# Attention, end of a head: the k-steps of r laid one by one between the samples' short products and behind their state products

## The chip, the cores and the metric

One core of one Trainium2 chip runs the whole program. The metric is the device time of one execution in microseconds. TensorE multiplies matrices into PSUM, VectorE and ScalarE work on SBUF and PSUM, GpSimd on SBUF, and SyncE issues most of the transfers. Each engine has its own queue of instructions, worked off in order; engines wait for each other by semaphores.

## The reference

A decoder layer runs for 1024 prompt tokens and for 8 samples of 8 tokens each. Its mixer holds a gated linear attention with 4 heads (key width 128, value width 256); a feed-forward part with product keys (PEER) gathers experts from memory and takes most of the time. What the changed stretch computes, cut from the reference:

```python
def step(s, inp):                       # one chunk of a head
    qi, ki, vi, gi = inp
    cum = jnp.cumsum(gi, axis=2)
    o_inter = jnp.einsum('bhcd,bhde->bhce', qi * jnp.exp(cum), s)
    ...                                 # scores with decay, inside the chunk
    o = o_inter + jnp.einsum('bhij,bhje->bhie', scores, vi)
    s_new = exp(last) * s + jnp.einsum('bhjd,bhje->bhde', ki * jnp.exp(last - cum), vi)
    return s_new, o
o = rms_norm(o, gla_norm_w)             # per head
o = o.reshape(bsz, t, GLA_DV) * jax.nn.silu(r)     # r = h @ w_in[:, r columns]
```

## The kernel before

`heads_phase` is a loop over the 4 heads. The 1088 tokens lie in 9 tiles: 8 of 128 prompt tokens, and a ninth (t = 8) with the 64 tokens of the samples. All work of a head on TensorE stands in one written order: the projections of q, k and v, the tile loop, and the end of the head. One more projection, r (256 output rows in two halves e, over 1088 tokens), isn't needed until the end of the head. It is cut into 6 pieces (half e, 384, 384 or 320 tokens), each of 8 k-steps; a k-step is three products with one block of 128 channels (high with high, high with low, low with high; L546 to L548). The 48 k-steps are laid as fillers into gaps of the other work: the list FILL says how many go to each place, and `fill(j)` writes those of place j. Place 0 is ahead of the tile loop, places 1 to 8 are in `results` of tiles 0 to 7 (behind the products L572, ahead of the state product L579), place 9 is after the samples' output products, and place 10 is after that.

All pieces use one PSUM bank (bank 7). When a piece's eighth k-step is done, ScalarE copies the bank to SBUF (`emptied`, L674) and only then may the next piece begin (`r_out`). ScalarE's own order is written out too: for each tile the output copy (L686), then `emptied` of that place, then the copy of the transposed keys (L698) and the exponentials of a tile two further on (L681).

The end of a head runs as follows. TensorE computes the samples' output: for each half e a product with the scores (L611), then for each of the 8 samples a product of its own state, 128 by 128, with only 8 columns (L614). Then comes the last filler. Then 8 state products (L627), one per sample, into two banks in turn; VectorE updates the sample's state from each (L797). Then six products (L633) sum the squares of the output over the channels. ScalarE makes these squares (the two activations L704 and L705, 1088 columns each), after the last `emptied`. After the sums come a root and a sigmoid on ScalarE, and the normalised output on VectorE, while TensorE goes on to the next head's q. When a head's third piece of r is complete, GpSimd splits the next head's q weights into a high and a low part (L144, L146); the k weights wait for all six pieces.

At the end of the phase all engines meet in a barrier, and the next phase starts then.

Of the kernel before, what the change touches and what calls it, by code (L numbers as in the profile page):

```python
# [15 lines left out]
KD = D // P  # L16
SEQ = 1024
NSEQ, LSEQ = 8, 8
T = SEQ + NSEQ * LSEQ
NC = 1 + NSEQ  # L20
NT = -(-T // P)
# [42 lines left out]
def col(t):  # L64
    return t * P if t < 2 else EARLY if t == NT - 1 else LATE + (t - 2) * P
# [302 lines left out]
def heads_phase(nc, A, G):  # L368


    with Scope(nc, "gla") as sc:
# [41 lines left out]
        M = {n: sc.sem(n) for n in names}  # L413
# [3 lines left out]
        tiles = [(t, rows(t), 0 if t < NT - 1 else 1) for t in range(NT)]  # L417
        assert NT % 2
        PIECES = [(e, t0, n) for e in range(2) for t0, n in TB]
        FILL = [KD] + [KD // 2] * (NT - 1) + [0, KD]  # L420
        filled = [sum(FILL[:j]) for j in range(len(FILL) + 1)]
        assert filled[-1] == len(PIECES) * KD
        r_bank = lambda p: PS[:, 7, 0:PIECES[p][2]]
# [71 lines left out]
        def _(pe):  # L495
# [3 lines left out]
            for b, (t0, n) in enumerate(TB):  # L499
                for kk in range(KD):  # L500
# [3 lines left out]
                    last = nc.tensor.matmul(PS[0:RANK, b, 0:n], lw_lo[:, kk, :], hi, start=False, stop=(kk == KD - 1))  # L504
            last.then_inc(M["low_mm"], 1)
            pe.wait_ge(M["low_ready"], 1)
            with pe.Fori(0, H) as i:
# [8 lines left out]
                for t, n, _ in tiles:  # L516
                    last = nc.tensor.matmul(PS[:, t // 4, t % 4 * DK:(t % 4 + 1) * DK],
                                            low[:, col(t):col(t) + P], w_alpha[:, bass.ds(i * DK, DK)],
                                            start=True, stop=True)
# [3 lines left out]
                for t, n, _ in tiles:  # L523
# [3 lines left out]
                    for kk in range(KD):  # L527
# [3 lines left out]
                        last = nc.tensor.matmul(out, lo, w_hi[:, 2:4, kk, :], start=False, stop=(kk == KD - 1))  # L531
# [1 line left out]
                pe.wait_ge(M["z_abs"], 2 * i + 2)  # L533
                pe.wait_ge(M["g_ready"], 4 * i + 4)

                def fill(j):

                    for s in range(filled[j], filled[j + 1]):
                        p, kk = divmod(s, KD)
                        e, t0, size = PIECES[p]  # L540
                        if kk == 0:
                            if t0 == 0:
                                pe.wait_ge(M["low_part"], NW * i + 5 + e)
                            pe.wait_ge(M["r_out"], 6 * i + p + 1)
                        hi, lo = h_hi[:, kk, t0:t0 + size], h_lo[:, kk, t0:t0 + size]
                        nc.tensor.matmul(r_bank(p), w_hi[:, e, kk, :], hi, start=(kk == 0), stop=False)  # L546
                        nc.tensor.matmul(r_bank(p), w_hi[:, e, kk, :], lo, start=False, stop=False)
                        last = nc.tensor.matmul(r_bank(p), w_lo[:, e, kk, :], hi, start=False, stop=(kk == KD - 1))  # L548
                        if kk == KD - 1:
                            last.then_inc(M["r_mm"], 1)  # L550
# [35 lines left out]
                for t, n, kind in tiles:  # L586
# [7 lines left out]
                    for l in range(LV + 1):  # L594
                        lhs = K[:, l, 0:n] if l < LV else k[:, col(t):col(t) + n]
                        rhs = Q[:, l, 0:n] if l < LV else q[:, col(t):col(t) + n]
                        last = nc.tensor.matmul(PS[0:n, 3 + l // 4, l % 4 * P:l % 4 * P + n], lhs, rhs,
                                                start=True, stop=True)
# [11 lines left out]
                for e in range(2):  # L610
                    last = nc.tensor.matmul(PS[:, 6, e * P:e * P + n], v[0:n, t, e * P:(e + 1) * P],  # L611
                                            sT[0:n, 0:n], start=True, stop=False)
                    for s in range(NSEQ):
                        last = nc.tensor.matmul(PS[:, 6, e * P + s * LSEQ:e * P + (s + 1) * LSEQ],  # L614
                                                Ss[:, s, e * P:(e + 1) * P],
                                                Qc[:, t % 3, s * LSEQ:(s + 1) * LSEQ],
                                                start=False, stop=(s == NSEQ - 1))
                last.then_inc(M["o_mm"], 1)
                fill(NT + 1)
                pe.wait_ge(M["kts"], i + 1)  # L620
                pe.wait_ge(M["masked"], NT * i + NT)
                for s in range(NSEQ):

                    pe.wait_ge(M["st_out"], NST * i + NT - 1 + max(s - 1, 0))
                    if s == 1:
                        pe.wait_ge(M["o_out"], NT * i + NT)
                    nc.tensor.matmul(ST if s % 2 else PS[:, 4, 0:DV], kTs[:, s, :], v[0:n, t, :],  # L627
                                     start=True, stop=True).then_inc(M["st_mm"], 1)
                pe.wait_ge(M["sq_ready"], i + 1)
                pe.wait_ge(M["st_out"], NST * (i + 1))  # L630
                for b, (t0, n) in enumerate(TB):
                    for e, src in enumerate((q, k)):
                        last = nc.tensor.matmul(PS[:, 3 + b, 0:n], G["ones"][:, :], src[:, t0:t0 + n],  # L633
                                                start=(e == 0), stop=(e == 1))
# [3 lines left out]
        def _(act):  # L638
# [6 lines left out]
            with act.Fori(0, H) as i:  # L645
# [23 lines left out]
                def emptied(j):  # L669

                    for p in range(filled[j] // KD, filled[j + 1] // KD):
                        e, t0, size = PIECES[p]
                        act.wait_ge(M["r_mm"], 6 * i + p + 1 + 6)
                        nc.scalar.activation(r[:, e, t0:t0 + size], r_bank(p), ACT.Copy).then_inc(M["r_out"], 1)  # L674
                def exps(t, n, kind):
                    act.wait_ge(M["e_mm"], NT * i + t + 1)
                    if t >= 2:
                        act.wait_ge(M["qk"], 3 * (NT * i + t - 2) + 3)
                    src = PS[:, 0:3, 0:384].rearrange("p b (l i) -> p b l i", l=3)[:, :, :, 0:n]
                    dst = E[:, t % 2].rearrange("p (b l) i -> p b l i", l=3)[:, :, :, 0:n]  # L680
                    nc.scalar.activation(dst, src, ACT.Exp).then_inc(M["e_exp"], 1)  # L681
                def output(t, n, kind):
                    act.wait_ge(M["o_mm"], NT * i + t + 1)
                    if t == 0:
                        act.wait_ge(M["o_free"], i + 1)
                    nc.scalar.activation(o[:, :, col(t):col(t) + n],  # L686
                                         PS[:, 6, 0:2 * P].rearrange("p (e i) -> p e i", e=2)[:, :, 0:n],
                                         ACT.Copy).then_inc(M["o_out"], 1)
# [3 lines left out]
                for t, n, kind in tiles:  # L692
                    if t >= 1:
                        output(*tiles[t - 1])
                        emptied(t)
                        act.wait_ge(M["st_mm"], NST * i + t)
                    act.wait_ge(M["t_mm"], NT * i + t + 1)
                    nc.scalar.activation(kT[0:n, :], PS[0:n, 5, 0:DK], ACT.Copy).then_inc(M["t_out"], 1)  # L698
                    if t + 2 < NT:
                        exps(*tiles[t + 2])  # L700
                output(*tiles[NT - 1])
                emptied(NT + 1)
                act.wait_ge(M["o_out"], NT * i + NT)
# [9 lines left out]
        def _(dve):  # L713
# [8 lines left out]
            with dve.Fori(0, H) as i:  # L722
# [17 lines left out]
                for gg, _, hi, lo in parts:  # L740
                    nc.vector.tensor_tensor(lo, gg, hi.bitcast(F32), ALU.subtract).then_inc(M["g_ready"], 1)
# [1253 lines left out]
def hybrid_decoder(nc, A):  # L1995

    with Scope(nc, "all") as top:
# [5 lines left out]
        with Scope(nc, "stream") as route:  # L2003

            G["h_hi"], G["h_lo"] = route.sb("h_hi", [P, KD, T], F32R), route.sb("h_lo", [P, KD, T], F32R)
            condition_phase(nc, A, G)
            heads_phase(nc, A, G)
# [115 lines left out]
```

## Time and profile before

| what | value |
|---|---|
| median of 3 runs | 4596.62 us (4596.38 to 4607.99) |
| the profiled execution's own time | 4599.16 us |
| its span, first to last instruction | 4597.4 us |
| PE busy | 3297.1 us, 72% |
| DVE busy | 2489.0 us, 54% |
| POOL busy | 1649.2 us, 36% |
| ACT busy | 803.6 us, 17% |
| mean granted TensorE clock | 0.784 of full speed |

The span is the program on the core; 1.8 us of the execution's own time lie around it. PE is TensorE's products, PEld its weight loads, DVE VectorE, ACT ScalarE, POOL GpSimd. The attention phase lies between about 160 and 725 us of the span. The granted clock is 1.00 at 2.4 GHz and 0.50 at 1.2 GHz. A product in full fp32 stands in the trace as two records, one in the rounded format (the k-steps, for one) as one. Records of TensorE overlap, since the next begins before the one ahead has drained; so the cost of one is read from start to start, not from its length.

### The profile page before, as it was taken

To read this page: it belongs to the slowest core of one execution; us is meant where nothing else is said; L and a number is where in the kernel's file an instruction comes from. 1 tells how busy PE (TensorE), PEld (TensorE's weight loads), DVE (VectorE), ACT (ScalarE), POOL (GpSimd) and SP (SyncE) were. 2 spreads that over 40 slices of the span, in tenths; PEclk is the share of its full clock that TensorE was granted. 3 is DMA by queue.
4 is the path that set the end of the run, shared out by engine and by line. 5 is a ranking of instruction groups with operands and counts; after the bars stand their busy time and mean duration, and the time that the engine had idled before them with its cause. 6 is when DMAs were issued, how large, how long until landed. Compare 5 with 4: busy or idle time off the path is not lost. (4 is left out here: it accounts for less than half of the span.)

```text
span 4597.4 us, 46652 instructions
## 1 busy us (share of the span) xinstructions
PE 3297.1 (72%) x15679; PEld 1688.6 (37%) x15679; DVE 2489.0 (54%) x7735; ACT 803.6 (17%) x1284; POOL 1649.2 (36%) x1379
## 2 busy tenths in 40 slices
PE   8899997736388666686768676667766666666676
PEld 2798896736055342351145334124211111111110
DVE  2245553126764445587755454557686555555555
ACT  2232233332113112110013211211000100000000
POOL 1211103523255343453345444344333333333332
PEclk9999998968599777797889888679766666666666
DMA  7211103533789889899889898999899999999998
GB/s 277 72 58 48 38 29 124 178 116 110 284 341 384 315 319 394 336 386 353 344 353 399 340 369 357 386 357 381 345 393 378 402 407 403 408 411 408 416 411 352
DMA packets 243431, 1400.14 MB, mean 305 GB/s; under 512 B 30662, under 2 KB 47686, under 8 KB 100987
## 3 DMA queue, kind: packets, MB, share of 16 engines
q0 software_dynamic: 156672, 1140.92, 61.9%
q1 hardware_dynamic: 86522, 256.22, 15.4%
q8 instruction: 131, 2.15, 0.2%
q14 instruction: 106, 0.86, 0.1%
HBM read 1345.59 MB, written 51.43 MB: 304 GB/s over the span
## 5 line engine op out<-in xcount | busy, mean ns | idle before, releaser
L1057 DVE CUSTOM_DVE_ANT_0 peer_uv<-peer_uv,all_PS 128x512 f32<-128x512 f32 x2176 | 1436.4, 685 | 1163.3 <-DMA peer_uv<-in_uv,peer_idx 782.8
L996 PE MATMUL all_PS<-peer_hT,peer_sel 96*128 96x512 bf16 x2176 | 1005.8, 486 | 1032.5 <-DVE peer_halves L1057 850.2
L979 POOL DMA_INDIRECT peer_uv<-in_uv,peer_idx x1088 | 1045.9, 961 | 1738.5 <-PE all_PS L1015 1360.4
L996 PEld LDWEIGHTS all_PS<-peer_hT,peer_sel 96*128 96x128 bf16 x2176 | 203.3, 102 | 2004.6 <-DVE peer_halves L1057 1623.6
L1015 PE MATMUL all_PS<-peer_uv,peer_zw 128*32 128x512 f32 x4352 | 878.0, 857 | 2.7 <-DVE peer_zw L1077 2.7
L867 POOL TENSOR_TENSOR flow_w_lo<-flow_w,flow_w_hi 128x1024 fp32r<-128x1024 f32 (+1 forms) x204 | 459.2, 2256 | 489.4 <-ACT flow_w_hi L860 488.9
L1031 ACT ACTIVATE peer_ge<-peer_pre 128x4 f32<-128x4 f32 x272 | 55.7, 205 | 2057.6 <-DVE peer_pre L1063 2057.5
L887 PE MATMUL all_PS<-mix_h_hi,flow_w_hi 128*128 128x384 f32 (+1 forms) x672 | 279.1, 415 | 33.2 <-POOL flow_w_lo L867 31.6
L860 ACT ACTIVATE flow_w_hi<-flow_w 128x1024 fp32r<-128x1024 f32 (+1 forms) x204 | 203.7, 1004 | 435.3 <-DMA flow_w<-in_w_proj_a 113.3
L888 PE MATMUL all_PS<-mix_h_lo,flow_w_hi 128*128 128x384 f32 (+1 forms) x672 | 225.2, 335 | 0.0
L889 PE MATMUL all_PS<-mix_h_hi,flow_w_lo 128*128 128x384 f32 (+1 forms) x672 | 225.1, 335 | 0.0
L1015 PEld LDWEIGHTS all_PS<-peer_uv,peer_zw 128*32 128x32 f32 x4352 | 109.5, 128 | 282.1 <-issue 279.0
L887 PE MATMUL all_PS<-keys_h_hi,flow_w_hi 128*128 128x384 f32 (+1 forms) x384 | 173.7, 452 | 27.7 <-DVE keys_h_lo L1682 27.7
L1057 DVE DVE_READ_ACCUMULATOR2_ANT peer_halves<- 128x1 f32 x2176 | 179.6, 83 | 0.0
L887 PEld LDWEIGHTS all_PS<-mix_h_hi,flow_w_hi 128*128 128x128 f32 x672 | 133.0, 198 | 104.4 <-issue 71.3
L144 POOL CAST gla_w_hi<-gla_w 128x1024 fp32r<-128x1024 f32 x24 | 24.9, 1038 | 374.2 <-PE all_PS L548 288.8
L888 PEld LDWEIGHTS all_PS<-mix_h_lo,flow_w_hi 128*128 128x128 f32 x672 | 131.4, 195 | 6.4
L888 PE MATMUL all_PS<-keys_h_lo,flow_w_hi 128*128 128x384 f32 (+1 forms) x384 | 130.2, 339 | 0.0
L889 PE MATMUL all_PS<-keys_h_hi,flow_w_lo 128*128 128x384 f32 (+1 forms) x384 | 130.1, 339 | 0.0
L889 PEld LDWEIGHTS all_PS<-mix_h_hi,flow_w_lo 128*128 128x128 f32 x672 | 130.0, 193 | 0.0
L1405 PE MATMUL all_PS<-flow_w_hi,out_x_hi 128*128 128x256 f32 (+1 forms) x288 | 107.1, 372 | 21.3 <-DVE out_x_lo L924 18.4
L887 PEld LDWEIGHTS all_PS<-keys_h_hi,flow_w_hi 128*128 128x128 f32 x384 | 77.6, 202 | 83.8 <-issue 83.5
(290 smaller groups left out, 4699.8 us busy)
## 6 DMA issues: line engine op xcount, KB each, us to landing
cond_w<-in_w_ada SPq DMA_DIRECT2D x12, 2048.0 KB, 8.2
flow_w<-in_w_gate_ab SPq DMA_DIRECT2D x48, 512.0 KB
flow_w<-in_w_query SPq DMA_DIRECT2D x48, 512.0 KB
flow_w<-in_w_conv SPq DMA_DIRECT2D x36, 512.0 KB
peer_uv<-in_uv,peer_idx POOLq DMA_INDIRECT x1088, 10.1
gla_w<-in_w_heads SPq DMA_DIRECT2D x24, 512.0 KB, 4.2
flow_w<-in_w_proj_b SPq DMA_DIRECT2D x24, 512.0 KB
flow_w<-in_w_out SPq DMA_DIRECT2D x24, 512.0 KB
```

Source lines behind the costliest of these rows:

```text
L144: nc.gpsimd.tensor_copy(hi, raw).then_inc(high, 1)
L860: nc.scalar.activation(self.hi[:, i % self.pairs, 0:nk], self.raw[:, i % self.raws, 0:nk], ACT.Copy).then_inc(self.high, 1)
L867: nc.gpsimd.tensor_tensor(self.lo[:, i % self.pairs, 0:nk], self.raw[:, i % self.raws, 0:nk], self.hi[:, i % self.pairs, 0:nk].bitcast(F32 ...
L887: nc.tensor.matmul(out, w_hi[:, k, :], x.hi[:, k, :], start=(k == 0), stop=False)
L888: nc.tensor.matmul(out, w_hi[:, k, :], x.lo[:, k, :], start=False, stop=False)
L889: last = nc.tensor.matmul(out, w_lo[:, k, :], x.hi[:, k, :], start=False, stop=(k == nk - 1))
L979: self.nc.gpsimd.indirect_dma_start(out=self.uv[:, n % self.NUV, :], out_offset=None, in_=self.A["uv"], in_offset=bass.IndirectOffsetOnAxi ...
L996: nc.tensor.matmul(PS[:, f, :], self.sel[:, c:c + 1].broadcast_to([3 * GR, P]), self.hT[:, g % self.NH, f * 512:(f + 1) * 512], start=True ...
L1015: last = nc.tensor.matmul(PS[j * GR:(j + 1) * GR, 2 + e, :], self.zw[:, z, GR - 1 - c:2 * GR - 1 - c], self.uv[:, n % self.NUV, D + e * 51 ...
L1031: nc.scalar.activation(self.ge[:, q % self.ND, :], self.pre[:, q % self.ND, :], ACT.Gelu_apprx_tanh).then_inc(M["gelled"], 1)
L1057: nc.vector.tensor_tensor_reduce(part, part, PS[:, f, :], 1.0, 0.0, ALU.mult, ALU.add, self.halves[:, d, f, e:e + 1]).then_inc(M["dotted"], 1)
L1405: nc.tensor.matmul(bank(j), x.hi[:, k, tok], w_hi, start=(k == 0), stop=False)
```

## The change

FILL changes from 8, eight times 4, 0, 8 to 8, eight times 3, 8, 8. Eight k-steps of r leave the tile loop, one from each place 1 to 8, and go to the end of the head. There, two places that were in one block are laid out singly. Place 9 puts one k-step behind each pair of the samples' 8-column products, and place 10 puts one behind each of the 8 state products; before, the last 8 stood in one block between the two groups. On ScalarE the copy of piece 4 now stands as `emptied(NT)`, ahead of the samples' output copy; that of the last piece stays in its place.

```diff
-        FILL = [KD] + [KD // 2] * (NT - 1) + [0, KD]
+        FILL = [KD] + [3] * (NT - 1) + [KD, KD]
...
-                def fill(j):
-
-                    for s in range(filled[j], filled[j + 1]):
+                def fill(j, first=0, last=2 * KD):
+
+                    for s in range(filled[j] + first, min(filled[j] + last, filled[j + 1])):
...
-                last.then_inc(M["o_mm"], 1)
-                fill(NT + 1)
+                        if e == 1 and s == NSEQ - 1:
+                            last.then_inc(M["o_mm"], 1)
+                        if s % 2:
+                            fill(NT, 4 * e + s // 2, 4 * e + s // 2 + 1)
                 pe.wait_ge(M["kts"], i + 1)
                 pe.wait_ge(M["masked"], NT * i + NT)
                 for s in range(NSEQ):
...
                     nc.tensor.matmul(ST if s % 2 else PS[:, 4, 0:DV], kTs[:, s, :], v[0:n, t, :],
                                      start=True, stop=True).then_inc(M["st_mm"], 1)
+                    fill(NT + 1, s, s + 1)
...
+                emptied(NT)
                 output(*tiles[NT - 1])
                 emptied(NT + 1)
```

The samples' output products on TensorE, before. L611 is the product with the scores, L614 the eight products with the samples' states (gla_Ss), L546 to L548 one k-step of r.

```order
L611 MATMUL all_PS<-gla_sT,gla_v 128x64
L614 MATMUL all_PS<-gla_Qc,gla_Ss 128x8 x8
L611 MATMUL all_PS<-gla_sT,gla_v 128x64
L614 MATMUL all_PS<-gla_Qc,gla_Ss 128x8 x8
L546 MATMUL all_PS<-stream_h_hi,gla_w_hi 128x320
L547 MATMUL all_PS<-stream_h_lo,gla_w_hi 128x320
L548 MATMUL all_PS<-stream_h_hi,gla_w_lo 128x320
```

Seven more k-steps of 320 columns follow there, and then the state products. The same place now:

```order
L611 MATMUL all_PS<-gla_sT,gla_v 128x64
L614 MATMUL all_PS<-gla_Qc,gla_Ss 128x8 x2
L546 MATMUL all_PS<-stream_h_hi,gla_w_hi 128x384
L547 MATMUL all_PS<-stream_h_lo,gla_w_hi 128x384
L548 MATMUL all_PS<-stream_h_hi,gla_w_lo 128x384
L614 MATMUL all_PS<-gla_Qc,gla_Ss 128x8 x2
L546 MATMUL all_PS<-stream_h_hi,gla_w_hi 128x384
L547 MATMUL all_PS<-stream_h_lo,gla_w_hi 128x384
L548 MATMUL all_PS<-stream_h_hi,gla_w_lo 128x384
```

Behind every second sample stands a k-step that was in the tile loop (384 columns).

The end of the head on TensorE, now. L629 is the state product (L627 before), L636 the sums of squares (L633 before); gla_q holds half of the squares.

```order
L629 MATMUL all_PS<-gla_v,gla_E 128x256
L546 MATMUL all_PS<-stream_h_hi,gla_w_hi 128x320
L547 MATMUL all_PS<-stream_h_lo,gla_w_hi 128x320
L548 MATMUL all_PS<-stream_h_hi,gla_w_lo 128x320
L633 REGISTER_ALU
L636 MATMUL all_PS<-gla_q,all_ones 128x384
```

The last k-step of r is now right ahead of the sums of squares; before, the eight state products stood between them.

The tile loop on TensorE, place 3, now. L572 is the product with the scores for tile 2.

```order
L572 MATMUL all_PS<-gla_sT,gla_v 128x128 x2
L546 MATMUL all_PS<-stream_h_hi,gla_w_hi 128x384
L547 MATMUL all_PS<-stream_h_lo,gla_w_hi 128x384
L548 MATMUL all_PS<-stream_h_hi,gla_w_lo 128x384
L546 MATMUL all_PS<-stream_h_hi,gla_w_hi 128x384
L547 MATMUL all_PS<-stream_h_lo,gla_w_hi 128x384
L548 MATMUL all_PS<-stream_h_hi,gla_w_lo 128x384
L544 REGISTER_ALU
L546 MATMUL all_PS<-stream_h_hi,gla_w_hi 128x320
```

A piece of r (384 columns) ends, and the next (320) begins, inside one place, with the wait for the bank's copy (L544) between them. With 4 steps at each place a piece always ended with its place. Place 6 has such a border too.

## Rows read from the trace of the kernel before

**Rows 1.** The page's part 4, shares of the span by engine, then by line.

```profile
DMA 13%; PE 5%; POOL 2%; issue 2%; DVE 1%; ACT 0%; POOLq 0%; ACTq 0%; DVEq 0%
DMA peer_uv<-in_uv,peer_idx 13%; PE all_PS L1015 3%; POOL peer_uv L979 2%; PE all_PS L996 2%; DVE peer_uv L1057 1%; DVE peer_halves L1057 0%; DVE peer_zw L1077 0%; DVE peer_y L1958 0%; ACT L1930 0%; ACT L1927 0%; DVE peer_y L1962 0%; POOLq L108 0%; ACT peer_y L1043 0%; ACT fin_root L1927 0%; ACTq L108 0%
```

**Rows 2.** Stretches, the four heads' ends: busy (instructions), clock, DMA share, GB/s.

```profile
272.00:296.00 24.00, 22.43 (x97) 0.79 0.19 73
411.00:436.00 25.00, 23.43 (x92) 0.73 0.18 70
550.00:575.00 25.00, 22.89 (x98) 0.80 0.18 69
689.00:711.00 22.00, 19.66 (x88) 0.84 0.14 54
```

**Rows 3.** Timeline of PE, second head's end: start, length, instructions, idle before.

```profile
412.12 0.43 PE L611 MATMUL all_PS<-gla_sT,gla_v 64*128 64x64 f32 x2 [0.57 <-DVE gla_S L765]
412.49 2.56 PE L614 MATMUL all_PS<-gla_Qc,gla_Ss 128*128 128x8 f32 x16
...
419.02 0.61 PE L546 MATMUL all_PS<-stream_h_hi,gla_w_hi 128*128 128x320 f32 x1
...
419.97 0.47 PE L546 MATMUL all_PS<-stream_h_hi,gla_w_hi 128*128 128x320 f32 x1
...
420.77 0.47 PE L546 MATMUL all_PS<-stream_h_hi,gla_w_hi 128*128 128x320 f32 x1
...
424.38 0.31 PE L546 MATMUL all_PS<-stream_h_hi,gla_w_hi 128*128 128x320 f32 x1
...
424.67 0.31 PE L548 MATMUL all_PS<-stream_h_hi,gla_w_lo 128*128 128x320 f32 x1
424.91 4.94 PE L627 MATMUL all_PS<-gla_v,gla_E 64*128 64x256 f32 x16
430.42 1.40 PE L633 MATMUL all_PS<-gla_q,all_ones 128*128 128x384 f32 x2 [0.57 <-DVE gla_Ss L797]
...
435.63 0.58 PE L135 MATMUL all_PS<-stream_h_hi,gla_w_hi 128*128 128x384 f32 x1
```

**Rows 4.** Stretches of the second head's end, columns as in rows 2.

```profile
414.00:416.00 2.00, 2.00 (x9) 0.50 0.00 0
...
426.00:428.00 2.00, 1.72 (x8) 1.00 0.00 0
```

**Rows 5.** Timeline of PE, first head's end.

```profile
273.37 1.95 PE L614 MATMUL all_PS<-gla_Qc,gla_Ss 128*128 128x8 f32 x16
275.25 0.43 PE L611 MATMUL all_PS<-gla_sT,gla_v 64*128 64x64 f32 x2
```

**Rows 6.** Line L627: what its engine waited for (us in four heads, times).

```profile
  DVE gla_Ss L797: 6.5, 12
```

**Rows 7.** Timeline of ACT, second head's end.

```profile
425.01 0.44 ACT L674 ACTIVATE gla_r<-all_PS 128x320 f32<-128x320 f32 x1 [5.53 <-PE all_PS L548]
425.35 1.10 ACT L704 ACTIVATE gla_q<-gla_o 128x1088 f32<-128x1088 f32 x1
426.35 1.10 ACT L705 ACTIVATE gla_k<-gla_o 128x1088 f32<-128x1088 f32 x1
```

**Rows 8.** Timeline of PE, second head's tile loop.

```profile
389.73 0.71 PE L568 MATMUL all_PS<-gla_Qc,gla_S 128*128 128x128 f32 x4 [1.66 <-DVE gla_S L765]
...
397.63 0.33 PE L546 MATMUL all_PS<-stream_h_hi,gla_w_hi 128*128 128x384 f32 x1
...
398.15 0.33 PE L546 MATMUL all_PS<-stream_h_hi,gla_w_hi 128*128 128x384 f32 x1
```

**Rows 9.** Timelines of DVE and POOL, the same loop.

```profile
381.45 0.15 DVE L751 COPY gla_decayed<-gla_E 128x1 f32<-128x1 f32 x1 [0.42 <-ACT gla_E L681]
...
386.00 2.68 POOL L146 TENSOR_TENSOR gla_w_lo<-gla_w,gla_w_hi 128x1024 fp32r<-128x1024 f32 x1
```

## The prediction

> **What bounds the kernel now.** I read the chain of waits first. Its largest lines are those of the feed-forward part (peer), where gathered experts set the pace, and all its shares together are a quarter of the span [rows 1]. It says nothing of the attention phase. That phase ends in a barrier, and what comes after starts then; so a microsecond won or lost at the end of a head should reach the end of the program, and I count it in full.
>
> Inside the phase I read TensorE's timeline at a head's end. It is busy nearly all of each of the four ends, with 1.5 to 2.3 us not busy in each, but its mean clock is 0.73 to 0.84 there [rows 2]. With two levels, a mean of 0.73 over 25 us is 25 x 0.27 x 2 = 13.5 us at 1.2 GHz. The four ends give 10.1, 13.5, 10.0 and 7.0 us. So TensorE sets the time of a head's end, partly at half speed.
>
> The second head's end in detail [rows 3]: the samples' output takes 412.12 to 419.02 = 6.90 us, the block of eight k-steps 5.89, the eight state products up to the sums 5.51, the sums of squares 5.21; 23.51 us in all. The clock stands at 0.50 during the short products and at 1.00 during the state products [rows 4]. TensorE had waited no more than 0.57 us ahead of them [rows 3]. What changed when it fell is that the array had 8 columns for each 128-column state it loads.
>
> At full clock eight short products take 275.25 - 273.37 = 1.88 us [rows 5]. Both halves are then 2 x (0.37 + 1.88) = 4.5 us, where 0.37 is L611 [rows 3]. A 320-column k-step takes 0.44 us at full clock (three products, 0.147 apart) and 0.80 at half [rows 3]; a 384-column one takes 0.52 [rows 8]. The block would take 8 x 0.44 + 0.23 = 3.75. Output and block together thus lost 12.79 - 8.25 = 4.54 us to some 10.2 us of low clock: 0.44 us per microsecond. (The 10.2 is the 13.5 less the 3.4 or so in the sums.)
>
> **The change part by part, per head.**
>
> *The tile loop.* Eight 384-column k-steps leave: 8 x 0.52 = 4.16 us less for TensorE. Two things take from it. First, two piece borders now lie inside a place. There TensorE stands still until the bank is copied. From the start of a piece's last product (424.67) to the start of the copy are 0.34 us, the copy takes 0.44 to 0.49, and I estimate 0.1 for the wake-up; less the 0.17 that the product takes anyway, the stall is 0.8 [rows 3, 7]. Two make 1.6, of which I let nothing hide. Second, VectorE waits for the exponentials only 0.42 us in such a tile [rows 9]. It can go along with three steps a place, but no further. So 4.16 - 1.6 = 2.6 us are won. The tile in which GpSimd's split (2.68 us) holds VectorE up and TensorE waits 1.66 us [rows 8, 9] comes two places later, since the third piece ends later; I expect it to be as long there as now. Ends for this term: 2.0 if VectorE becomes the bound, 3.4 if the borders hide under its work (8 x 0.42).
>
> *The samples' output.* Now per pair: two short products 0.47, a k-step 0.52, and a change of weights of about 0.1 (the block's first product lasts 0.61 against 0.47 [rows 3]), of which half may hide. That is 1.03 us; with the two L611, 8 x 1.03 + 0.74 = 9.0 us, if the clock holds. Ends: 8.6 with all loads hidden, 10.3 with 0.2 per pair exposed.
>
> *The state products.* The border ahead of piece 5 is not hidden. The first state product (0.43) covers half of the 0.8, so 0.4 us are left. Then eight rounds of a state product and a k-step. The eight products now take 5.51 us, of which 0.57 is the wait ahead of the sums and 6.5 / 4 = 1.6 waits for VectorE [rows 3, 6]; that leaves 0.42 each. With 0.44 and 0.1 for changing weights (0.24 from the last k-step to L627 [rows 3], against 0.147) a round is 0.97. VectorE's waits vanish under the k-step. Sum: 0.4 + 7.7 = 8.1 us.
>
> *The wait that the change adds.* ScalarE makes the squares after its copy of the last piece, and the sums need the squares. Now the state products cover copy and squares. With the last k-step right ahead of the sums, nothing covers them: from 424.67 + 0.31 to 426.35 + 1.10 are 2.5 us [rows 3, 7]. From the last product's start it is 2.8 us with a wake-up, less the 0.15 that the rounds already hold: 2.7 us. Behind it on TensorE's queue stand the sums and the next head's q; behind the sums, the root, the sigmoid and the last products on VectorE. GpSimd's split of the next k weights also waits for the last piece, but it has the sums and the whole q projection as cover; I cost it at nothing. ScalarE's earlier copy of piece 4 moves its output copy by a microsecond; TensorE needs that only at the second state product, behind a border and a k-step. Nothing there either.
>
> *The sums.* They took 5.21 us in the second head, with a fall of the clock around them. After 2.6 us of standing still I expect the same in all four heads; the ends are 3.8 (never low) and 6.4 (low throughout).
>
> Sum for the second head: 9.0 + 8.1 + 2.7 + 5.2 = 25.0 against 23.5, so 1.5 more. The other heads were faster before, having less low clock [rows 2]: by 0.44 x 3.4, 0.44 x 3.5 and 0.44 x 6.5 us, that is 1.5, 1.5 and 2.9. So the ends grow by 1.5 + 3.0 + 3.0 + 4.4 = 11.9 us, and the loops shrink by 4 x 2.6 = 10.4. Net +1.5 us if the clock holds in the new output stage. Ends by the bounds: about -9 and +9.
>
> **Does the clock hold there?** No row of before shows a k-step among short products. By rows the new stage lies between. Short products alone, 8 columns in 0.235 us, let it fall. The state products, whose 0.42 of work filled two thirds of the time, ran at 1.00 [rows 4]; yet near their end the clock fell in this head, for the sums take 5.21 us and their first matmul 1.40 for two records. In the new stage the array works 0.5 of each 1.03 us, and its start is thin: 0.57 us of waiting, L611, then two short products. If the clock falls there, nothing in the stage brings it back soon: at half speed a pair costs 2 x 0.43 + 3 x 0.32 + 0.15 = 2.0 us, and the array is busy half of that. I estimate 5 us more for the rest of the output (5.5 pairs at 0.95) and 3 to 6.5 for the rounds (0.80 - 0.44 and 0.43 more in each): 8 to 12, I take 10 us for each head in which it falls. I expect this in none or in one head of the four.
>
> The Trainium skill (TensorE: Matmul & The Clock Gate, "Why this matters for your kernels") says that the clock drops when TensorE idles between bursts of matmuls. By that rule alone the new stage would hold it in all heads, and only the wait for the squares could endanger it; the sum would then be +1.5 us. The trace speaks against the rule's being enough: the clock was at 0.50 in short products that had at most 0.57 us of idling ahead of them [rows 3, 4].
>
> The same page ("Step-by-step: what each phase is for") says that TensorE's queue loads weights ahead of a running matmul. By that, one load of each pair hides under the k-step in front of it, 0.1 us at most; the low end 8.6 would hold and the sum be 1.6 us lower.
>
> **Forecast.** +1.5 us with no fall, +11.5 with one; I take +6. Against the profiled execution (span 4597.4, own time 4599.16) that is 4605; the profile lies 2.5 us above the median of 4596.62, so the median to come is 4603.
>
> **Rivals.**
>
> *A: the clock falls in the output stage in two or more heads.* Place: behind L611. Price: 10 us a head; it decides from the second head on, since 1.5 + 20 = 21.5 us is past the bound. For it: the clock fell around this stage in all four heads before [rows 2], and the stage's start is as thin as it was. Against it: 3 x 384 + 16 columns in 1.03 us, where the short products alone send 8 in 0.235. Time: 4618 to 4638.
>
> *B: the waits hide and the clock gains.* The borders go under VectorE's work (another 0.8 a head), the loads hide (0.4), and the sums run at full clock (1.4): 1.5 - 4 x 2.6 = -8.9 us, 4588. For it: two of the ends had less low clock. Against it: the wait for the squares is as sure as ScalarE's order.
>
> *C: the change does not reach the time.* Order and records move, but the start of the next phase is set by ScalarE and VectorE after the last head, and in between by the next head's exponentials. Then 4596 to 4598. Against it: TensorE is hardly idle in the heads' ends.
>
> **Chances.** Forecast 0.58 (own range 4594 to 4612), A 0.25, B 0.12, C 0.05. A change of 0.3% is 13.8 us, about what a measurement of this kernel can tell from none. The forecast lies within it but for its upper end (0.07 of the 0.58 is slower). Its sum and the bounds of its terms leave a third of B, 0.04, past the bound. So faster 0.04, same 0.64, slower 0.32. For 8 in 10 the range goes from 4590, which cuts off half of B, to 4624, which takes in the fall in two heads and cuts off three and four.
>
> **What would show it.** (1) TensorE idle about 2.5 us ahead of the sums (L636), put down to ScalarE's squares, in every head; if it is under 1 us, I misread ScalarE's order. (2) In places 3 and 6 idle stretches of about 0.8 us behind ScalarE's copy of r, four or more in all. (3) Clock 1.00 in most of the output stages, each about 9.0 us long; about 16 us and 0.50 where it falls. (4) Rounds of state product and k-step 0.97 us apart, with no wait for VectorE. (5) A tile loop shorter by 2 to 3.4 us a head. The prediction is wrong if the ends grow by less than 6 or more than 25 us in total, or if time moves outside the attention phase by more than some 5 us.

## The result and the profile after

The changed kernel takes 4614.74 us, the median of 20 runs (4597.18 to 4637.4), against 4605.74 (4594.72 to 4624.06) for 20 runs of the kernel before beside it. The ratio is 1.0025, with a 95% interval of 1.0014 to 1.0037: 0.25% slower, some 11.5 us (6 to 17); the two medians are 9.0 us apart. That is under the 0.3% that I had set as the bound of "same", and inside the range.

The profiled execution took 4609.81 us, its span 4608.0. Here are the four heads' ends as stretches (busy, instructions, mean clock, DMA share, GB/s), against [rows 2]:

```profile
272.00:301.00 29.00, 25.82 (x120) 0.94 0.15 53
412.00:441.00 29.00, 25.82 (x120) 0.94 0.13 49
549.00:578.00 29.00, 25.82 (x121) 0.94 0.12 46
688.00:731.00 43.00, 39.08 (x114) 0.56 0.07 28
```

Three ends run at 0.94 instead of 0.73 to 0.80, so the clock holds there but for a few us in the sums. They are longer all the same: from L611 to the end of the last sum 27.3 us each. Before, the four took 22.1, 23.9, 22.2 and 20.7. The fourth fell to half speed and took 41.4 us.

TensorE's timeline in the second head's end, against [rows 3]:

```profile
413.26 0.43 PE L611 MATMUL all_PS<-gla_sT,gla_v 64*128 64x64 f32 x2 [0.57 <-DVE gla_S L769]
413.62 0.61 PE L614 MATMUL all_PS<-gla_Qc,gla_Ss 128*128 128x8 f32 x4
414.09 0.42 PE L546 MATMUL all_PS<-stream_h_hi,gla_w_hi 128*128 128x384 f32 x1
...
415.06 0.42 PE L546 MATMUL all_PS<-stream_h_hi,gla_w_hi 128*128 128x384 f32 x1
...
422.17 0.70 PE L629 MATMUL all_PS<-gla_v,gla_E 64*128 64x256 f32 x2
...
425.97 0.70 PE L629 MATMUL all_PS<-gla_v,gla_E 64*128 64x256 f32 x2
426.59 0.41 PE L546 MATMUL all_PS<-stream_h_hi,gla_w_hi 128*128 128x320 f32 x1
...
427.23 0.70 PE L629 MATMUL all_PS<-gla_v,gla_E 64*128 64x256 f32 x2
...
432.03 0.31 PE L548 MATMUL all_PS<-stream_h_hi,gla_w_lo 128*128 128x320 f32 x1
434.94 0.99 PE L636 MATMUL all_PS<-gla_q,all_ones 128*128 128x384 f32 x2 [2.60 <-ACT gla_k L709]
```

Three things are to be seen. A pair of short products with its k-step takes 0.97 us (415.06 - 414.09), the whole output stage 8.9. A round of state product and k-step takes 1.26 us (427.23 - 425.97); 0.62 of it pass before the k-step begins. And TensorE stands still for 2.60 us ahead of the sums, put down to ScalarE's second square. Its waits over the phase (us in total, times, longest):

```profile
PE all_PS L636 <- ACT gla_k L709: 10.4, 4, 2.6
PE all_PS L558 <- ACT gla_E L684: 7.5, 4, 1.9
PE all_PS L546 <- ACT gla_r L677: 4.8, 8, 0.6
PE all_PS L568 <- DVE gla_S L769: 0.9, 3, 0.3
```

The first row is new, and so is the third, the border inside a place, twice a head. The second row is the same as before (7.5 us). The fourth is TensorE's wait behind the tile that GpSimd's split holds up. It was this before, so 4.1 us of the wait are gone:

```profile
PE all_PS L568 <- DVE gla_S L765: 5.0, 3, 1.7
```

In the last head the clock fell in the third pair of the output stage and stayed down until the last of the sums. From one of its rounds to the next:

```profile
702.92 1.22 PE L629 MATMUL all_PS<-gla_v,gla_E 64*128 64x256 f32 x2
704.77 0.47 PE L548 MATMUL all_PS<-stream_h_hi,gla_w_lo 128*128 128x320 f32 x1
705.17 1.22 PE L629 MATMUL all_PS<-gla_v,gla_E 64*128 64x256 f32 x2
```

A round there takes 2.25 us. In the eight rounds no product of TensorE had to wait, and yet they didn't bring the clock back.

From the second tile (its L591) to L611, the loop takes 47.0 us in three heads and 46.5 in the last, against 50.9 and 49.0. The balance at the last sum of the last head (730.3 against 710.2 us): ends +34.3, of which the one fall is 14.1; loops -14.1; the projections between heads -3.8; a later start of the first loop +3.7. That is +20. The span grew by only 10.6. The rest of the program took 9.5 us less in this execution than in the one before. Differences of that size come by chance: a second trace of the same changed kernel reaches its last sum at the same point (729.6) and has a span 19 us longer (4627.2).

### The profile page after: what moved, and what is told of

Read it like the earlier page. It is cut to its first block and busy times, and to the rows that moved or that the text cites. A ratio compares the mean times of both kernels' runs of the same rounds, so it can differ in the third digit from the quotient of the medians.

```text
span 4608.0 us, 46652 instructions
## 1 busy us (share of the span) xinstructions
PE 3305.2 (72%) x15679; PEld 1687.5 (37%) x15679; DVE 2488.5 (54%) x7735; ACT 803.7 (17%) x1284; POOL 1644.5 (36%) x1379
## 5 line engine op out<-in xcount | busy, mean ns | idle before, releaser
L1019 PE MATMUL all_PS<-peer_uv,peer_zw 128*32 128x512 f32 x4352 | 864.3, 844 | 2.5 <-DVE peer_zw L1081 2.5
L144 POOL CAST gla_w_hi<-gla_w 128x1024 fp32r<-128x1024 f32 x24 | 25.2, 1050 | 378.3 <-PE all_PS L548 301.2
## 6 DMA issues: line engine op xcount, KB each, us to landing
peer_uv<-in_uv,peer_idx POOLq DMA_INDIRECT x1088, 10.1
flow_w<-in_w_proj_b SPq DMA_DIRECT2D x24, 512.0 KB, 11.2
```

The costliest lines, as they stand in the source:

```text
L144: nc.gpsimd.tensor_copy(hi, raw).then_inc(high, 1)
L1019: last = nc.tensor.matmul(PS[j * GR:(j + 1) * GR, 2 + e, :], self.zw[:, z, GR - 1 - c:2 * GR - 1 - c], self.uv[:, n % self.NUV, D + e * 51 ...
```

## The experiments

Readings from one trace each, in us per head (four values where they differ); the last column of times, "ends", is the sum of the four heads. "Ends" is from L611 to the last sum; "out" the part up to the first state product, "states" from there to the sums. The ratio is to the kernel before, with its 95% interval. The changed kernel was not timed beside these versions, so a distance to it is the quotient of two ratios, uncertain by about 0.2% or 10 us either way.

| kernel | loop | out | states | sums | ends | ratio |
|---|---|---|---|---|---|---|
| before | 50.9, last 49.0 | 9.7, 12.8, 12.7, 11.2 | 5.5 to 5.6 | 6.8, 5.6, 3.9, 3.9 | 88.9 | 1 |
| changed | 47.0, last 46.5 | 8.9, last 14.0 | 12.8, last 20.6 | 5.6, last 6.7 | 123.2 | 1.0025 [1.0014, 1.0037] |
| squares first | 47.0, 46.5 | 8.9, last 13.8 | 10.1, last 17.8 | 3.9, last 4.9 | 105.3 | 0.9982 [0.9964, 1.0000] |
| full rows | 47.0, 46.5 | 8.8 | 10.15 | 5.4 to 5.6 | 98.1 | 0.9984 [0.9963, 1.0005] |
| states only | 50.9, 49.0 | 4.5, 6.7, 4.5, 5.1 | 20.6 | 5.6 to 6.6 | 127.4 | 1.0081 [1.0053, 1.0109] |
| samples only | 47.0, 46.5 | 13.3, third 20.7 | 5.5 (6.5) | 5.6 to 7.0 | 107.5 | 0.9998 [0.9979, 1.0018] |
| borders | 47.1, last 44.9 | 8.9 | 12.8 | 5.6 to 6.6 | 110.2 | 1.0076 [1.0057, 1.0095] |
| step ahead | 47.4, last 46.8 | 8.3 | 12.8 | 5.6 to 6.6 | 108.3 | 1.0010 [0.9995, 1.0025] |
| thin | 47.0, 46.4 | 9.7, 8.9, 8.9, 11.4 | 20.6, 12.8, 12.8, 20.6 | 5.6 to 6.3 | 129.3 | 1.0043 [1.0026, 1.0061] |
| four edits | 49.0, 47.4, 47.4, 45.3 | 8.2 | 7.35 | 3.9 | 77.9 | 0.9953 [0.9939, 0.9968] |
| four edits less one | 47.4, last 46.8 | 8.2 | 7.35 | 3.9 | 77.9 | 0.9944 [0.9929, 0.9959] |

**Squares first.** ScalarE's order alone:

```diff
-                emptied(NT + 1)
                 act.wait_ge(M["o_out"], NT * i + NT)
                 nc.scalar.activation(q[:, :], o[:, 0, :], ACT.Square)
                 nc.scalar.activation(k[:, :], o[:, 1, :], ACT.Square).then_inc(M["sq_ready"], 1)
+                emptied(NT + 1)
```

> The changed kernel, with ScalarE's two squares ahead of its copy of r's last piece instead of behind it; nothing else moves. Theory W (the wait ahead of the sums, 2.6 us a head in the changed kernel, is ScalarE's squares alone): last k-step to sums falls from 2.91 to about 0.3 us, the stretch from the first state product to the sums from 12.8 to 10.2 us, and, with TensorE no longer idle there, the clock stays at 1.00 in the sums, which take 3.8 to 3.9 instead of 5.6 us. About 4 x 4.3 = 17 us less than the changed kernel, so some 6 us under the kernel before. Rival V (another wait stands right behind it: the eighth state's update on VectorE, or the bank's copy): the wait shrinks by less than 0.5 us a head, and the time moves by 2 us at most.

Measured: last k-step to sums 0.25 us, the states' stretch 10.1, the sums 3.9, in the three heads at full clock. TensorE's timeline there:

```profile
425.16 0.30 PE L548 MATMUL all_PS<-stream_h_hi,gla_w_lo 128*128 128x320 f32 x1
425.41 0.91 PE L636 MATMUL all_PS<-gla_q,all_ones 128*128 128x384 f32 x2
```

and ScalarE's, with both squares done seven microseconds before the last copy:

```profile
416.09 1.11 ACT L707 ACTIVATE gla_q<-gla_o 128x1088 f32<-128x1088 f32 x1
417.11 1.10 ACT L708 ACTIVATE gla_k<-gla_o 128x1088 f32<-128x1088 f32 x1
425.50 0.44 ACT L677 ACTIVATE gla_r<-all_PS 128x320 f32<-128x320 f32 x1 [7.29 <-PE all_PS L548]
```

Theory W holds: 4.3 us a head in those three, 2.65 of waiting and 1.7 of clock in the sums behind it. In the last head the output stage had fallen, as in the changed kernel. By the ratios the version is 0.43% under the changed kernel, some 20 us (10 to 30) for 17 forecast.

**Full rows.** The state products contract over 128 rows instead of 64. The rows added to the masked keys are zero.

```diff
-        kTs = E[0:TAIL, 1, 0:NSEQ, :]
+        kTs = E[:, 1, 0:NSEQ, :]
...
-                                        seq_rows[:, :, None].broadcast_to([n, NSEQ, DK]),
+                                        seq_rows[:, :, None].broadcast_to([P, NSEQ, DK]),
...
-                    nc.tensor.matmul(ST if s % 2 else PS[:, 4, 0:DV], kTs[:, s, :], v[0:n, t, :],
+                    nc.tensor.matmul(ST if s % 2 else PS[:, 4, 0:DV], kTs[:, s, :], v[:, t, :],
```

> The changed kernel, with the state products contracted over 128 rows instead of 64 (the added rows are zero in the masked keys). Theory R (a round of state product and k-step takes 1.26 instead of the forecast 0.97 us because weights of 64 rows are not loaded ahead while a product over 128 rows runs, nor the other way): the load of the state product's weights starts right behind the k-step's last product, and a round takes 0.95 to 1.0 us, 2.2 us a head less, 9 us in all. Rival D (the 0.19 us of idle ahead of each state product is a wait for VectorE's update, as the trace names it, and the rest is the product's own length): rounds stay at 1.2 to 1.26 us and the time does not move. The samples' output and the tile loop are as in the changed kernel.

Measured: rounds of 0.87 us, 0.39 less than with 64 rows and even under the forecast. The loads of weights (PEld) in the changed kernel:

```profile
426.85 0.19 PEld L548 LDWEIGHTS all_PS<-stream_h_hi,gla_w_lo 128*128 128x128 f32 x1
427.23 0.29 PEld L629 LDWEIGHTS all_PS<-gla_v,gla_E 64*128 64x128 f32 x2 [0.19 <-DVE gla_Ss L801]
427.85 0.19 PEld L546 LDWEIGHTS all_PS<-stream_h_hi,gla_w_hi 128*128 128x128 f32 x1 [0.33 <-issue]
```

and with full rows:

```profile
419.18 0.19 PEld L548 LDWEIGHTS all_PS<-stream_h_hi,gla_w_lo 128*128 128x128 f32 x1
419.32 0.34 PEld L629 LDWEIGHTS all_PS<-gla_v,gla_E 128*128 128x128 f32 x2
419.68 0.19 PEld L546 LDWEIGHTS all_PS<-stream_h_hi,gla_w_hi 128*128 128x128 f32 x1
```

The two idle stretches, 0.19 and 0.33 us, are gone. The wait instruction for VectorE is the same in both kernels, so the name in the first row misleads: the load did not begin ahead of time behind a product over another number of rows. Theory R is shown for this pair of shapes. By the ratios the time is 0.41% under the changed kernel, 19 us (8 to 30), where Theory R has 9. The excess is not explained, but it is inside the error. This trace has no fall of the clock, and its phase ends 9 us before that of the changed kernel's one trace without a fall.

**States only.** The kernel before, with only its last eight k-steps behind the state products (`fill(NT + 1, s, s + 1)`), and nothing else changed.

> The kernel before, with only its last eight k-steps laid one by one behind the state products; the tile loop keeps four k-steps a place, and the short products stand alone as before. Theory C (the clock falls in the short products, and rounds of state product and k-step do not bring it back): the clock is at 0.50 from the short products to the sums, a round takes about 2.25 us, and a head's end takes 8 to 12 us more than before, 30 to 45 us in all. Rival H (rounds are dense enough to bring the clock back within a few us): rounds of 1.26 us after at most 4 us, a head's end 1 to 4 us longer than before (squares' wait 2.6 us included), 4 to 16 us in all.

Measured: 0.81% or 37 us slower than the kernel before, and its phase ends 39 us later. All four ends run at 0.56 to 0.63 of full clock, with rounds of 2.25 us and the squares' wait of 2.60. In the first and third head the clock fell only as the rounds began, since their output stages took the 4.5 us of full clock. The second head:

```profile
428.85 1.22 PE L626 MATMUL all_PS<-gla_v,gla_E 64*128 64x256 f32 x2
430.70 0.47 PE L548 MATMUL all_PS<-stream_h_hi,gla_w_lo 128*128 128x320 f32 x1
431.10 1.22 PE L626 MATMUL all_PS<-gla_v,gla_E 64*128 64x256 f32 x2
...
449.50 1.64 PE L633 MATMUL all_PS<-gla_q,all_ones 128*128 128x384 f32 x2 [2.60 <-ACT gla_k L705]
```

Theory C holds: before, the clock came back within the block of k-steps, and the rounds don't bring it back. Whether rounds with full rows would is not tested, for no trace of them starts from a fallen clock. This half of the change is harmful without the other half, with which the clock held in most heads.

**Samples only.** The changed kernel with the last eight k-steps in one block ahead of the state products (`fill(NT + 1)` before the wait for `kts`).

> The changed kernel, with its last eight k-steps in one block ahead of the state products, as before the change; the tile loop and the k-steps between the short products stay as changed. Theory W + R (squares' wait and rounds are the two losses of the changed kernel): output stage 8.9 us, border of 0.6 to 0.8, block 3.7, state products 5.5 to the sums with a wait of 0.57, so about 19 us up to the sums instead of 21.7; 2.7 us a head less than the changed kernel, 11 us in all, level with or some 5 us under the kernel before. Rival K (what the change gains lies in the rounds, which cover VectorE's updates): 19 us is not reached, the time rises above the changed kernel.

Measured: 13.26 + 5.51 = 18.8 us up to the sums in two heads, as forecast; 19.7 in the last, where the clock fell in the state products. In the third it fell in the output stage, which took 20.7 with its block, and came back in the block. Level with the kernel before (0.9998), so 0.27% or 12 us under the changed kernel, for 11 forecast. Theory W + R holds for its size.

**Borders.** `FILL = [KD, 4, 4, 3, 3, 2, 3, 3, 2, KD, KD]`.

> The changed kernel, with the 24 k-steps of the tile loop shared out as 4, 4, 3, 3, 2, 3, 3, 2 instead of 3 eight times, so that every piece ends with its place. Theory B (a border inside a place costs 0.8 us of standing still, twice a head): no idle stretch behind ScalarE's copy in the loop, the loop falls from 47.0 to 45.6 to 46.0 us, 4 to 5 us less in all. Rival D (VectorE bounds the loop there, or the tile with GpSimd's split takes it back): the tiles with 3 or 2 steps stay at 5.57 us, the loop shortens by less than 0.5 us, and the time does not move. With the wait gone, GpSimd's split may also meet VectorE's sums of products again, as in the kernel before (a tile of 8.3 us), and the loop would be 1 us longer.

Measured: the theory fails as a gain, in the way that the last sentence of the expectation names. The waits are gone, and the last head's loop is 1.5 us shorter. In the three others one tile takes 8.04 to 8.14 us, since VectorE's L784 stretches from 1.15 to 3.31 us under GpSimd's split. VectorE's row in the second head:

```profile
392.95 3.31 DVE L784 TENSOR_TENSOR gla_soft<-gla_soft 128x512 f32<-128x512 f32 x2
```

and GpSimd's, which starts 0.05 us before it:

```profile
392.90 2.35 POOL L146 TENSOR_TENSOR gla_w_lo<-gla_w,gla_w_hi 128x1024 fp32r<-128x1024 f32 x1
```

In the changed kernel the split comes behind a border, at a point where TensorE is late anyway. VectorE's rows there:

```profile
399.41 1.13 DVE L761 TENSOR_TENSOR gla_Ss<-gla_E,gla_k 128x128 f32<-128x128 f32 x1
400.46 1.21 DVE L779 TENSOR_TENSOR gla_soft<-all_PS,gla_pairs 128x1024 f32<-128x1024 f32 x1
401.70 2.14 DVE L784 TENSOR_TENSOR gla_soft<-gla_soft 128x512 f32<-128x512 f32 x2
```

L761 loses about 0.85 us to the split's first instruction (L144, which ends at 400.39) and L784 1.0 to the second. L779, whose input is in PSUM, loses nothing. And TensorE waits 0.31 behind them instead of the 1.66 of [rows 8]. The measured time, 35 us above the kernel before by the ratio and 28 by the medians, is more than this trace explains. So I took a second one:

> The version whose pieces end with their places, again. Its runs lay 28 us above the kernel before, yet its trace shows no fall of the clock in the output stages. Theory T: in most of its runs two or three heads fall, which its traced run was spared; this trace has one or more long ends (39 to 42 us). Rival M (the time is lost outside the attention phase): ends of 27.3 us, a phase that ends near 732 us, and a span above 4620 us.

It has two ends of 41.4 us at clock 0.55 (out 14.1 and 14.0, rounds 2.25), and its phase ends 29 us later than in the first trace. That accounts for such times. The trace shows one thing more. In the same two heads, the first and the third, the clock had already fallen inside the tile loop, behind the split, and the tile took 9.7 and 9.6 us instead of 8.05. The first head, TensorE's wait and the clock behind it:

```profile
254.05 0.71 PE L568 MATMUL all_PS<-gla_Qc,gla_S 128*128 128x128 f32 x4 [2.10 <-DVE gla_S L769]
```

```profile
255.00:257.00 2.00, 2.00 (x9) 0.55 0.00 0
257.00:259.00 2.00, 2.00 (x8) 0.59 0.00 0
259.00:261.00 2.00, 2.00 (x19) 1.00 0.04 8
```

The clock was back before the output stage began, and fell there again. In the changed kernel this wait is 0.31 us and no trace has a fall there. Whether the first fall brings on the second, and whether this version falls more often at all, stays open; six runs and two traces don't tell.

**Step ahead** and **thin** change the start of the output stage. The first writes `fill(NT, 0, 1)` ahead of the wait for VectorE's state, and the others one pair earlier. The second puts two k-steps behind every fourth short product.

> The changed kernel, with the first k-step of place 9 ahead of the wait for VectorE that precedes the samples' output, and the others each one pair earlier, none behind the last pair. Theory T (the clock falls where the stage begins thinly: waiting, the product with the scores, two short products): TensorE works through the 0.57 us of waiting, the stage takes 8.9 - 0.5 = 8.4 us from L611, and the clock is at 1.00 in the output stage of all four heads. Rival U (the whole stage is thin enough, its start makes no difference): the clock falls in one head in four or more, as in the changed kernel's trace.

> The changed kernel, with two k-steps behind every fourth short product of the output stage instead of one behind every second; the same work, a thinner start. Theory T (the thin start decides): the clock falls in more heads than the one of the changed kernel, in two to four, each costing 13 to 14 us; 15 to 40 us above the changed kernel. Rival U (the mean over the stage decides, and it is unchanged): none or one head falls, and the time is that of the changed kernel within 5 us.

Step ahead: 8.3 us out in all four heads (its first k-step now stands ahead of L611, where the loop is 0.35 us longer), no fall, and 0.15% under the changed kernel. Thin: two of four heads fell, with ends of 36.6 and 38.2 us, so 9 and 11 us each where theory T had 13 to 14; by its time it is 8 us above the changed kernel, less than the 15 that theory T had as its low end. Neither time is apart from the changed kernel's beyond the error. The traces lean to theory T, but each is one trace of something that depends on chance. So two more of the changed kernel:

> The changed kernel again, unchanged, for a second trace. Theory T (whether the clock falls in an output stage is chance, about one head in four, and costs 13 to 14 us each): the heads' ends are either 27.2 to 27.3 us or 39 to 42 us long, nothing between; none to two are long, not necessarily the last head's. Rival L (the last head is special, its clock always falls): again the last head alone.

> The changed kernel once more, for a third trace; expectations as for the second.

The first has one long end, the second head's, 41.4 us; all others are 27.3. The second has none (27.1 to 28.3; the 28.3, which the expectation left no room for, is a last head whose sums took 6.6). Rival L is out. Here are the stretches of the first one:

```profile
272.00:300.00 28.00, 25.30 (x117) 0.94 0.15 51
411.00:453.00 42.00, 39.38 (x117) 0.55 0.11 41
565.00:593.00 28.00, 24.92 (x115) 0.94 0.13 50
702.00:730.00 28.00, 24.69 (x112) 0.94 0.11 43
```

Counted over all traces: with the changed kernel's output stage, 6 of 32 heads fell in it (two of the six in the second trace of "borders"); with a k-step ahead, 0 of 12 (the two four-edit versions included); thinner, 2 of 4. If all had the same chance of 6 in 32, 12 heads without a fall would still happen about one time in twelve. So that the step ahead protects is likely, not shown.

**Four edits, and four less one.** Squares first, full rows, step ahead and borders together; then without the borders.

> The changed kernel with four edits together: squares ahead of the last copy, pieces that end with their places (4, 4, 3, 3, 2, 3, 3, 2), one k-step ahead of the samples' output, and state products over 128 rows (the added ones zero). If each does what it did or would do alone: loop 45.8, output stage 8.4, states 7.4 to the sums (12.8 less 2.65 and 2.6), sums 3.9; 65.5 us a head from the second tile on, where the kernel before has 72.9, 72.9, 72.9 and 69.6 by its own trace. So 4 x 6 to 7 = 25 to 28 us under the kernel before, at full clock throughout. Rival: the time saved at the ends is lost again behind them, in the wait for the next head's weights (GpSimd's split) or in the phases that follow, and the kernel is less than 10 us faster.

> The four-edit version with the tile loop of the changed kernel (three k-steps at every place, borders inside places 3 and 6). The loop takes 47.4 us in three heads and 46.8 in the last, against 49.0, 47.4, 47.4 and 45.3; the ends 19.5 us each, all at full clock. So level with the four-edit version within 2 us, and 20 to 27 us under the kernel before. Rival: GpSimd's split meeting VectorE costs more than the borders in other runs too, and this version is 4 us or more faster than the four-edit one.

Measured: 0.47% (22 us) and 0.56% (26 us) under the kernel before. The ends take 19.5 us each, at full clock in every head of both traces. The stretches of the second version:

```profile
268.00:288.00 20.00, 19.69 (x112) 1.00 0.01 2
400.00:420.00 20.00, 19.66 (x111) 1.00 0.01 2
533.00:553.00 20.00, 19.86 (x113) 1.00 0.01 2
665.00:686.00 21.00, 20.04 (x113) 1.00 0.14 57
```

The first version kept slightly less than its expectation of 25 to 28 us. Its loops are 5.9 us longer in all than the 45.8 each that I had put in: the split stretches VectorE's products again in three heads (tiles of 8.05 us), and in the first head the clock also fell behind it, as in the second "borders" trace (a tile of 9.6 us). The second version is 4 us faster, as its rival said, but their intervals overlap, so the borders edit is worth nothing within the error. The second version is the one to keep.

## Why the prediction was right, and where it was not

The sign of the balance, its size within the bound, and its shape were right: the loops win, the ends lose, and one head in about six (two of twelve in three traces) loses its clock. The size was forecast as +6 us and measured as +11.5. By its steps:

- *The tile loop.* Forecast 2.6 us won a head, ends 2.0 to 3.4. Measured 3.9 in three heads and 2.5 in the last. The last has no split of a next head's weights, and there the sum was right. In the others it failed in one sentence, that the tile with GpSimd's split would be as long at its new place. Before, the split made a loop 1.9 us longer than the last head's (50.9 against 49.0), now it is 0.5 (47.0 against 46.5). The tile with the border at place 6 takes 6.5 us with the split and without, where the tile with the split took 8.3; only the tile behind it is longer with the split, 6.05 against 5.5. Both borders cost what was said: without them the last head's loop is 1.5 us shorter, so 0.8 each.
- *The samples' output.* Forecast 9.0, measured 8.9, with 0.97 us a pair for 1.03. The rule of the Trainium skill (TensorE: Matmul & The Clock Gate, "Step-by-step: what each phase is for") on loading weights ahead went with a low end of 8.6; the trace lies nearer to my sum.
- *The border ahead of piece 5.* Forecast 0.4. The state product, longer than thought, hid it: the first round takes 1.28 for 1.26. With full rows it is there, 1.28 against 0.87.
- *The rounds.* Forecast 0.97, measured 1.26, so 2.3 us a head too little, 9 in all. This is the term that was mis-sized. I took VectorE's waits out of the old 5.51 us and gave 0.1 for changing weights. In fact, at each change between 128 and 64 rows the next weights were not loaded ahead, which full rows shows by 0.87.
- *The wait for the squares.* Forecast 2.5 us from the last product's end, measured 2.60; removed alone, it gave back what it should. The sums behind it took 5.6 in the three heads by the table, which counts to the last record's end, and 5.21 to the next head's first product (440.15), for 5.2 forecast. In the last head of the third trace, without a fall, they took 6.6, so "the same in all four" did not quite hold.
- *The clock.* "None or one of four" came true in all three traces (1, 1, 0). The price was 14.1 us, not 10: 5.1 in the output, 7.9 in the rounds, 1.1 in the sums. The forecast had 3 to 6.5 for the rounds, at most 0.79 us for each; they stayed slow all eight, at 0.99 each (2.25 against 1.26).

Without a fall the phase ends 3.7 us later than before (the third trace, 713.9 against 710.2 us at the last sum), where +1.5 was forecast. That this came so close is luck. In that trace the ends grew by 21.1 us for 11.9 forecast, mostly the rounds. The loops shrank by 14.0 for 10.4, and the projections between the heads and the start of the first loop took 3.4 us less, which I had at nothing. So 9.2 too little was made good by 3.6 and 3.4. Two falls in twelve heads add 0.67 x 14.1 = 9.4 us on average, where I had taken 5. That makes 13, where the ratio says 11.5. The upper end of +9 without a fall was also not the sum of the bounds: with the sums' own 6.4 it would have been about +14.

By two of my own tests the prediction is wrong. The ends were to grow by 6 to 25 us in all, and in the profiled execution they grew by 34.3 (34.3 again in the second trace, 21.1 in the third). The ends failed it because the rounds and the price of a fall were both too low, and with both right, one fall is already past 25. The other test was time moving outside the phase by more than 5 us. In the profiled pair it moved by 9.5. That test was badly set, as the repeated trace shows: the rest of the program varies by about 20 us between executions of one kernel.

Rival A did not come true in the traces. The slowest runs (to 4637) would fit two falls, but none of its three traces has two, and the rest of the program alone varies by 20 us. Rival B had the right idea of what could be won, but not by itself: it took squares first and full rows. Rival C is out, since a later or earlier end of the phase reached the program's time: 39 us later in the trace and 37 us more in "states only", 25 us earlier and 26 us less in the last version.

## What to carry to other kernels

When filler work is moved behind the last covered piece of a stage, look at what the engines that serve it do in order: here ScalarE's squares stood behind a copy that had just become the last thing to be ready, and putting the squares ahead of the copy gave back more (some 20 us) than the whole change had cost (11.5). A filler only pays where changing to it and back is cheap, so measure one round. And where a low clock is what a change is after, price both outcomes by the rows at each level, and take several traces, for one doesn't tell the chance.

## What the runs showed of the hardware

- In the rounds, weights of 64 rows were not loaded while a product over 128 rows ran, nor weights of 128 rows while one over 64 rows ran (0.19 and 0.33 us without a load); with 128 rows for both they were. Padding the short contraction with zero rows made a round 0.39 us shorter (1.26 to 0.87).
- A fallen clock stayed down through eight rounds, 20.6 us without a wait between TensorE's products, in one head's end of the changed kernel (37.5 us at half speed in all, the 2.60 us wait and most of the sums included), and in all four ends of the version with states only. Before, and in the third head of "samples only", it came back within a block of eight k-steps.
- GpSimd's subtraction (2.35 to 2.68 us long) held up VectorE's sums from SBUF by 1.0 to 2.6 us, depending on when they met it, and its conversion ahead of that (1.14 us) a product from SBUF by 0.85. Neither held up the product with an operand in PSUM (L779 took 1.21 us, as always).
- The clock also fell in three tile loops, each time behind a wait of some 2 us for VectorE, and stayed down for 3.4 us; in six other loops with the same wait it held.
